# Down weights of the expert blocks loaded through ScalarE's DMA queue in place of SyncE's

## The reference, cut to what matters

```
for e in range(N_EXPERTS):                       # 16 experts, D_MODEL 1024, D_EXPERT 512
    he = silu(t @ w_gate[e]) * (t @ w_up[e])     # t: (512, 1024)
    y = y + gates[:, e:e + 1] * (he @ w_down[e])
```

## Time and profile before

| | |
|---|---|
| median of 3 runs | 1894.25 us (1891.43 to 1902.06) |
| the profiled execution | 1893.68 us |
| its span | 1891.8 us |
| mean granted TensorE clock, share of full | 0.893 |
| expert blocks of the first layer | about 607 to 930 us of the span |
| expert blocks of the second layer | about 1546 to 1868 us of the span |

### The profile page before, as it was taken

One profiled execution on the slowest core, in us unless ns is written; L12 is line 12 of the kernel. 1 busy time (PEld: TensorE's weight loads), 2 busy tenths in 40 slices (PEclk: granted clock), 3 DMA queues, 4 the chain that ended last, 5 costly groups with the idle time before them and its releaser, 6 DMA issues. The chain is left out here.

```text
span 1891.8 us, 19071 instructions
## 1 busy us (share of the span) xinstructions
PE 1602.9 (85%) x6262; PEld 1038.1 (55%) x6262; DVE 1245.6 (66%) x1771; ACT 808.2 (43%) x1151; POOL 464.7 (25%) x210
## 2 busy tenths in 40 slices
PE   6997998769965899999479979986799758999992
PEld 3443453644544678787334434546445456778781
DVE  2494586732256799999435936867222559999993
ACT  2413324421144677777123123244301447777860
POOL 0000131300000456665300001312000005656542
PEclk9998999569986999999779989995699869999996
DMA  5231301301302899998711311031103048999974
GB/s 184 79 89 34 112 1 43 113 1 46 134 0 99 299 396 398 398 395 333 257 34 34 89 34 34 1 91 65 47 1 133 1 156 307 394 399 396 398 306 172
DMA packets 153799, 307.54 MB, mean 163 GB/s; under 512 B 35030, under 2 KB 48252, under 8 KB 153612
## 3 DMA queue, kind: packets, MB, share of 16 engines
q1 hardware_dynamic: 142044, 264.18, 39.3%
q0 software_dynamic: 6912, 25.17, 3.6%
q10 hardware_dynamic: 4784, 17.45, 2.3%
HBM read 280.02 MB, written 27.93 MB: 163 GB/s over the span
## 5 line engine op out<-in xcount | busy, mean ns | idle before, releaser
L494 PE MATMUL ps<-hT,arena 128*128 128x512 f32 (+2 forms) x768 | 354.5, 617 | 1.6 <-DVE hT L793 1.6
L1514 POOL TENSOR_TENSOR rest_w_down<-arena,head_w_down 128x2048 fp32r<-128x2048 f32 x32 | 216.6, 6769 | 137.2 <-ACT head_w_down L1601 137.2
L494 PEld LDWEIGHTS ps<-hT,arena 128*128 128x128 f32 (+2 forms) x768 | 141.5, 189 | 195.5 <-issue 192.3
L1659 DVE TENSOR_TENSOR rest_w_down<-arena,head_w_down 128x2048 fp32r<-128x2048 f32 x32 | 159.7, 4991 | 6.7 <-ACT head_w_down L1601 6.7
L1659 DVE TENSOR_TENSOR rest_w_up<-arena,head_w_up 128x2048 fp32r<-128x2048 f32 x64 | 143.4, 2281 | 1.3 <-ACT head_w_up L1601 1.3
L1659 DVE TENSOR_TENSOR rest_w_gate<-arena,head_w_gate 128x2048 fp32r<-128x2048 f32 x60 | 134.6, 2284 | 0.6 <-issue 0.6
L1546 PE MATMUL ps<-head_w_gate,xg_head 128*128 128x512 f32 x256 | 106.4, 416 | 32.6 <-DVE xg_rest L1665 32.6
L1601 ACT ACTIVATE head_w_up<-arena 128x2048 fp32r<-128x2048 f32 x64 | 120.5, 1963 | 0.0
L1601 ACT ACTIVATE head_w_down<-arena 128x2048 fp32r<-128x2048 f32 x64 | 118.8, 1909 | 1.3 <-issue 1.3
L1546 PE MATMUL ps<-head_w_down,he_head 128*128 128x512 f32 x256 | 104.2, 407 | 15.8 <-POOL rest_w_down L1514 15.8
L1462 POOL DMA_INDIRECT xg<-hrows,slot_tok x2 | 4.9, 2429 | 456.7 <-DVE slot_tok L1436 456.7
(11 more groups left out here) (275 smaller groups left out, 3006.6 us busy)
## 6 DMA issues: line engine op xcount, KB each, us to landing
arena<-in_w_gate SPq DMA_DIRECT2D x64, 1024.0 KB, 8.1
arena<-in_w_up SPq DMA_DIRECT2D x64, 1024.0 KB, 8.2
arena<-in_w_down SPq DMA_DIRECT2D x64, 1024.0 KB, 7.1
yrows<-yb ACTq DMA_DIRECT2D x32, 512.0 KB, 6.4
arena<-in_w_in SPq DMA_DIRECT2D x10, 1536.0 KB, 6.7
arena<-in_w_in SPq DMA_DIRECT2D x4, 2048.0 KB, 8.7
arena<-in_w_in SPq DMA_DIRECT2D x20, 256.0 KB, 5.1
arena<-in_w_out SPq DMA_DIRECT2D x2, 2560.0 KB, 17.7
```

What stands on the lines that cost most here:

```text
L494: last = nc.tensor.matmul(ps[n % 3][0:width, :], w[:, c, col:col + width], hT[:, c, :], start=(c == 0), stop=(c == KD - 1))
L1514: nc.gpsimd.tensor_tensor(wl[2][:, c, :], raw[2][:, c, :], wh[2][:, c, :].bitcast(F32), ALU.subtract)\
L1659: nc.vector.tensor_tensor(wl[q][:, c, :], raw[q][:, c, :], wh[q][:, c, :].bitcast(F32), ALU.subtract)\
```

## The change

SyncE no longer loads down weights in the loop and after it. ScalarE does, through a new function `load_down`, with the same two waits for each load, now in ScalarE's sequence: at the top of iteration k, ahead of `head(0, k+2)`, it loads the down weights of block k+1, once the raw buffer's content of block k has been subtracted. The first block's down weights are still loaded by SyncE.

```diff
                     with sp.Fori(1, last_two_out(sp)) as k:
                         load(0, k + 2, k + 1)
                         load(1, k + 2, k + 1)
-                        load(2, k + 1, k)
-                    load(2, block_count(sp), last_two_out(sp))
                     if l + 1 < L:
...
+                    def load_down(n, before):
+                        e = act.value_load(blki[0:1, bass.ds(n - 1, 1)], min_val=0, max_val=E - 1)
+                        src = A["w_down"][l:l + 1, bass.ds(e, 1)].rearrange("o e (c p) n -> p (o e c) n", p=P)
+                        for j in range(2):
+                            act.wait_ge(*split(2, j, before))
+                            act.dma_start(raw[2][:, part(2, j), :], src[:, part(2, j), :]).then_inc(s_raw[2][j], 16)
+
...
                     with act.Fori(1, last_two_out(act)) as k:
+                        load_down(k + 1, k)
                         head(0, k + 2, k + 1)
                         rows_head(0, k + 2)
                         rows_head(1, k + 2)
...
                         silu(k + 2)
+                    load_down(block_count(act), last_two_out(act))
                     h_head(block_count(act))
```

## The result

The changed kernel takes 1938.95 us in the median of 4 runs (1935.91 to 1943.89), against 1893.55 us of 4 runs of the kernel before: a ratio of 1.0245, 95% interval 1.0221 to 1.0270. It is slower by 45.4 us between the medians. The forecast was 1937 us.

What follows compares the result with a forecast made beforehand. The loop was taken as bound by a VectorE-TensorE circle of 18.50 us, not by transfers. ScalarE's moved wait adds 1.65 us in 26 periods, 42.9 us on 1893.68: 1936.6, taken as 1937 us, range 1922 to 1954.

Steps and rivals of the forecast that it cites:

- The bound: Block loops: a circle of `gated`, gate subtractions, `rows_rest`, then gate and up matmuls closes the 18.50 us period; no transfer in it.
- The turn of GpSimd and VectorE: Down subtractions in each period: after VectorE's second up half, 4.48 us of GpSimd, then 2.16 us of VectorE.
- The rival in which GpSimd went first between the up halves: GpSimd's down half runs before VectorE's second up half, delaying VectorE's down half: 117 us more, 2011 us; chance 0.02.
- What is removed, 0: SyncE's two waits and two issues per down load go away; the next gate load doesn't wait for them: worth 0.
- The faster rival: SyncE's order is the bound, so gate and up loads come earlier: 14 us saved, 1880 us; chance 0.03.
- What is added, 1.65 us a period: ScalarE's first gate head, behind the moved wait and issue, starts 4.95 us late; 3.30 us of slack cover part.
- How often, 26: First of 14 iterations covered, thirteen pay, in two layers: 26 × 1.65 = 42.9 us.
- TensorE's clock: Full grant expected at 2.2 us idle per period; rival with a third of gate and up at 1.2 GHz: 1991 us, chance 0.03.
- The two queues: Down loads on ScalarE's queue share the same 16 DMA engines; down halves have more cover than before: 0.
- The wait holds no activation: Rival: on ScalarE's queue the gate heads pass the waiting load, so all stays as now: 1894 us; chance 0.04.

Runs made afterwards that it cites:

- both_edits: The kernel before, with VectorE subtracting the rows' rest between the two gate halves and doing both down halves, GpSimd none: 1871.92 us, ratio 0.9895.
- load_after_gate_head: The changed kernel with the whole `load_down` moved from before `head(0, k+2)` to behind it: 1892.76 us, ratio 1.0003 to the kernel before.
- first_half_only: The changed kernel with ScalarE loading only the first half of the down weights, SyncE the second as before: 1892.56 us, ratio 1.0002 to the kernel before.
- waits_only: The kernel before, SyncE still issuing every down load, with only the two waits put at the top of ScalarE's loop: 1930.01 us, ratio 1.0196.

## Why the prediction was right, point by point

**The bound.** Right. The circle of `gated`, gate halves, rows and matmuls was the loop; moving one gate half out of it shortened the period, and relieving GpSimd alone did not. The transfers were rightly called no part of the wait, but the prediction didn't see how near they were. The 379 GB/s of the earlier trace rows take in the end of the loop, where hardly anything is loaded any more; from 673 to 877 us the kernel before moved 397, and both_edits, with transfers in its waits, 398.

**The turn of GpSimd and VectorE.** Right, and settled by the run in which VectorE does both halves. This case agrees with the Trainium skill (*SBUF — State Buffer*, "Who interferes with whom") that the loser waits for the whole instruction: with GpSimd out of it, VectorE's down half takes 2.2 us and not 4.92. The rival in which GpSimd went first between the up halves didn't occur in any period read.

**What is removed, 0.** Right: load_after_gate_head and first_half_only, which also take down loads off SyncE, are at 1.000. The faster rival falls with them.

**What is added, 1.65 us a period.** The mechanism held: the head behind the wait, the slack used up, then the full rest of the delay in every period. The size was 1.77. The term that was mis-sized is "the next activation follows an issue on ScalarE by 0.04": it was 0.19 behind a weight load (805.31 to 805.50). The issue was 0.38 for 0.37, the handover to VectorE 1.95 for 1.99. So t to the gate subtraction is 2.68 us, forecast 2.56, and 26 × 1.77 = 46.0 for 42.9. The trace shows what stands in the missing 0.15 us. Between the issue's end and the head, ScalarE's sequence computes the values that the head's two waits compare with:

```profile
L1596 ACTq FUSED_REGOPS  x1: 37/37/37, 805.3 to 805.3; - x1
...
L1598 ACTq ALU_OP  x1: 41/41/41, 805.4 to 805.4; - x1
```

Between the store's issue and `silu`, where the 0.04 was read, the trace has no such instruction, and in the kernel before the head's register work ran beside `silu` and cost nothing.

**How often, 26.** Right. At the first iteration of the first layer the gate subtraction starts 0.43 us behind `gated` and waits for nobody, as in the earlier trace rows:

```profile
645.30 4.49 DVE L1666 TENSOR_TENSOR rest_w_gate<-arena,head_w_gate 128x2048 fp32r<-128x2048 f32 x2 [0.43 <-issue]
```

**TensorE's clock.** Half wrong. The prediction took full grant at a 2.2 us gap, because it was nearer to 1.65; at 2.31 us the grant fell in six periods, and in waits_only at gaps of 1.8 to 1.9 us in eight, so the 1.65 us of one row could not vouch for it. Its rival priced a fall of a third of gate and up in every period, 55 us more; in fact `gated` came 1.6 us late in those six, and the 1.68 us of cover took it. The forecast's number survived because of the cover, which its own walk had left (1.6 us) but not meant for this: in that point it was luck.

**The two queues.** Right: cover grew and nobody waited. The rule of the Trainium skill (*DMA: Bandwidth & Descriptors*, "Issuing engines are not separate DMA queues") agrees with all the runs, also where transfers bind: 400 GB/s before the move there, and no time won by it.

**The wait holds no activation.** Fell with waits_only.

## What to carry to other kernels

A load moved to another engine's queue brings its wait along, and that wait stands in front of everything the engine does next; so compare the moment of the event with the latest start of the next instruction, and put the load behind the work that the event would hold. Here one place cost 46 us over 26 periods, and the next line down cost nothing. When the loop closes through several nearly full resources, a delay beyond the slack is paid in full in every period, while what is below it is free.

## What the runs showed of the hardware that was not expected

- A DMA issue on ScalarE with an address from a register holds the sequence longer than its own 0.38 us: with 0.16 us of register work ahead of it and 0.41 of issue, the second issue behind t made a period 0.60 us longer. The next activation's own register work, 0.19 us before it starts, comes on top where nothing covers it.
- ScalarE's queue runs ahead of its activations: the first down load was issued at 789.22 us while the two gate heads of 786.88 to 790.59 were running. That is why a load behind them isn't late.
- The grant of TensorE's clock can fall to half behind an idle gap of 2.3 us in a loop that is otherwise busy, in six of 28 periods, and behind one of 1.8 to 1.9 us in eight of 28; with a gap of 1.4 us it fell in none.
- In every kernel here with a mean period of at most 18.5 us the block loop moved 396 to 399 GB/s (673 to 877 us), the kernel before included, and neither the second queue nor another order of work gave more.
